# Recurrence of a two-block model: both head groups take the block inverse in step, on 32 columns

## The chip, the cores and the metric

One NeuronCore of a Trainium2 chip runs the whole program. The metric is the device time of one execution in microseconds (us), lower is better; a kernel is given by the median of several executions. PE is TensorE (PEld its loads of weights, the stationary operand), DVE is VectorE, ACT is ScalarE, POOL is GpSimd and SP is SyncE.

## The reference, cut to what matters

The model is a stack of four layers and then a second block, all on 512 tokens of 1024 channels. Only one piece of the second block is touched by the change, the RWKV-7 recurrence over 16 heads of 64 channels:

```python
def step(state, inp):
    r_t, w_t, k_t, v_t, a_t, b_t = inp
    sa = jnp.einsum('bhij,bhj->bhi', state, a_t)
    state = state * w_t[:, :, None, :] + sa[..., None] * b_t[:, :, None, :] \
        + v_t[..., None] * k_t[:, :, None, :]
    return state, jnp.einsum('bhij,bhj->bhi', state, r_t)
_, ys = lax.scan(step, jnp.zeros((B, H, N, N), jnp.float32), xs)
```

All the rest (the projections, the MLPs, the attentions, the norms) stays as it was.

## The kernel before, in words

**The whole.** Nearly all the time goes to large projections whose weights stream in and are split into an upper and a lower part (lines 435 and 440), and which PE multiplies in three float32r terms (line 505). Every engine runs one written-out program, and semaphores order them. The recurrence stands between the stage `g2` and the stage `mattn`: `pe_chunks`, `act_chunks`, `dve_chunks` and `pool_heads` (line 2216). No other work of PE runs inside it.

**The recurrence in chunks.** The 512 tokens are cut into 8 chunks (NC) of 64 (CH). Within a chunk the step by step scan becomes matrices of 64 by 64 for each head, and the sequential part becomes the inverse of a unit triangular matrix. The 16 heads lie as pairs (h, k): h is the half of the 128 partitions, k the column block 0 to 7. Group 0 is k = 0 to 3, group 1 is k = 4 to 7. Group 1 keeps its tokens in the other half of the partitions (`toks`, line 1875) than its channels (`chan`, line 1871), so that products of tokens into channels use the quadrants of PE's array that group 0 leaves free. `together` (line 1879) issues the products of one or more groups turn by turn. A float32 product is two instructions on PE, so one product for all the heads of a group is 16 matmuls, and for both groups 32.

**The inverse.** It is built by levels of doubling blocks. X and Z hold the inverse so far and its transpose. `first_x` and `first_z` (lines 1962 and 1963) make level 0, for blocks of 2. Level l = 1 to 5 does three products: `times` (line 1993) multiplies the masked matrix TM with X to give Y, `more_x` (line 1964) multiplies Z with Y and VectorE adds the result to X (`add_x`, line 2178), and `more_z` (line 1965) adds into Z's PSUM bank (6 and 2, ZB), which ScalarE copies to SBUF (`act_z`, line 2080). X and Y share the PSUM banks 4 and 5 (YX). ScalarE copies Y to SBUF as Yt (`act_y`, line 2084). Level 5 makes no X. The masks `mk` leave in TM only the source rows and target columns that join two neighbouring blocks of 2 to the power l, so a product has only 32 of 64 columns that change, but before the change all 64 are computed and copied.

**The order of the work.** The two groups go staggered: PE does `times` of group 0, then `more_x` and `more_z` of group 1 for the level before, then other work, then `more_x` of group 0, then `more_z` of group 0 with `times` of group 1. The other work lies in the middle of a level, while the copies of Y and Z run: at l = 1 the turning of the next chunk's V and B (`pe_turn`, line 1890), at l = 2 the head sums of the chunk before (line 1916) and `w0_tok` (line 1967), at l = 3 `w0_state` (line 1969) and the head spread (line 1924), at l = 4 the products with B of the next chunk (`pe_products`, line 1900), at l = 5 the turning of its K. After level 5 come U (line 1971), with the products with K of the next chunk between its two groups, then `o_v`, `ds_b`, `ds_k`, `o_u` and `o_state` (lines 1975, 1972, 1973, 1977, 1979). The next chunk's `first_x` follows at once; its `first_z` waits until ScalarE has copied the output out of ZB (semaphore `ck_out`, line 2127). The last chunk has no next one, and its levels 1, 4 and 5 lack the other work.

**VectorE in a chunk** copies X (line 2189), updates the state (`state`, lines 2173 to 2175), adds X, makes the masked TM (`level`, line 2151, 512 elements), masks the products with B (`mask_b`) and K (`mask_k`, both line 2146), makes the first level of the next chunk (lines 2163 and 2164), and scales the finished heads (line 1947). POOL then finishes those heads.

## Time and profile before

| what | value |
|---|---|
| median of 3 executions | 3448.69 us (3445.75 to 3448.97) |
| the profiled execution, its own time | 3444.75 us |
| its span in the profile | 3442.9 us |
| instructions | 51687 |
| granted TensorE clock, mean | 0.993 of full speed |
| PE, PEld busy | 98%, 80% of the span |
| DVE, ACT, POOL busy | 51%, 34%, 14% |
| the recurrence, from first_x of chunk 0 to the end of chunk 7 | 2633.5 to 2853.5 us |

The profile gives busy times per engine; matmuls overlap in their pipeline, so the busy time is the union of intervals and their ends are modelled. The timeline of the trace lists instructions in order of start with their count, and in brackets the idle time of that engine before them and what ended it. A start to start distance on PEld is the best clock for how fast PE goes through a burst of products.

### The profile page before, as it was taken

Reading aid. Unit: us, or ns where it says so; the run is one execution under the profiler, and the core shown is the slowest. Engines: PE = TensorE matmul, PEld = TensorE weight load, DVE = VectorE, ACT = ScalarE, POOL = GpSimd, SP = SyncE. Lnnn points to the kernel's source line nnn. Section 1 sums busy time; section 2 is a strip of 40 time slices with the busy share of each in tenths; the row PEclk is TensorE's granted clock in tenths of the full one; section 3 lists DMA queues with packets and bytes.
Section 4 is the critical chain, followed back from the end, with each engine's and each line's share of the span. In section 5 each row is a group of like instructions: output and inputs, shape, how many; then the busy total and the mean of one; then the engine's idle time right before and its main releaser. Section 6 shows DMA issues by size and latency. Waiting matters only on the chain. (4 is left out here: it accounts for less than half of the span.)

```text
span 3442.9 us, 51687 instructions
## 1 busy us (share of the span) xinstructions
PE 3368.9 (98%) x21556; PEld 2754.1 (80%) x21556; DVE 1754.3 (51%) x1916; ACT 1161.5 (34%) x1452; POOL 465.4 (14%) x420
## 2 busy tenths in 40 slices
PE   8999999999999999999999999999998989999998
PEld 6688888888888888888588888887777877878887
DVE  7764343454345554345765243555686554554342
ACT  3532223432222232222532123334663542342122
POOL 1011011020011021011011012100141221111011
PEclk9999999999999999999999999999999999999999
DMA  4233233232322233233233323343332122313232
GB/s 144 68 105 103 87 98 99 85 98 98 98 98 89 95 100 103 91 98 117 71 97 97 99 96 110 112 131 114 107 96 82 41 65 97 112 61 108 88 100 71
DMA packets 313223, 329.56 MB, mean 96 GB/s; under 512 B 22707, under 2 KB 303670, under 8 KB 312534
## 3 DMA queue, kind: packets, MB, share of 16 engines
q1 hardware_dynamic: 306069, 303.33, 27.7%
q0 software_dynamic: 4464, 19.40, 1.7%
q10 hardware_dynamic: 2512, 4.26, 0.3%
q8 instruction: 137, 2.24, 0.3%
q14 instruction: 41, 0.33, 0.0%
HBM read 312.28 MB, written 14.68 MB: 95 GB/s over the span
## 5 line engine op out<-in xcount | busy, mean ns | idle before, releaser
L505 PE MATMUL ps<-xh,wh 128*128 128x512 f32 x2360 | 930.7, 394 | 9.4 <-DVE wl L440 7.2
L505 PE MATMUL ps<-xh,wl 128*128 128x512 f32 x2360 | 920.3, 390 | 0.0
L505 PE MATMUL ps<-xl,wh 128*128 128x512 f32 x2360 | 919.9, 390 | 0.0
L440 DVE TENSOR_TENSOR wl<-raw,wh 128x2048 fp32r<-128x2048 f32 (+1 forms) x279 | 636.6, 2282 | 425.6 <-ACT wh L435 425.3
L435 ACT ACTIVATE wh<-raw 128x2048 fp32r<-128x2048 f32 (+1 forms) x281 | 526.2, 1873 | 639.8 <-PE ps L505 627.2
L505 PEld LDWEIGHTS ps<-xh,wh 128*128 128x128 f32 x2360 | 444.2, 188 | 114.5 <-issue 21.3
L505 PEld LDWEIGHTS ps<-xl,wh 128*128 128x128 f32 x2360 | 444.1, 188 | 95.6 <-issue 4.6
L505 PEld LDWEIGHTS ps<-xh,wl 128*128 128x128 f32 x2360 | 443.9, 188 | 92.9
L505 PE MATMUL ps<-hh,wh 128*128 128x512 f32 x1280 | 498.5, 389 | 1.1 <-DVE wl L440 0.9
L505 PE MATMUL ps<-hh,wl 128*128 128x512 f32 x1280 | 498.0, 389 | 0.0
L505 PE MATMUL ps<-hl,wh 128*128 128x512 f32 x1280 | 497.9, 389 | 0.0
L621 POOL TENSOR_TENSOR hf<-tmp 128x512 f32<-128x512 f32 x160 | 163.2, 1042 | 1133.7 <-DVE tmp L668 1133.7
L588 ACT ACTIVATE hh<-tmp 128x512 f32 (+1 forms) x160 | 97.8, 633 | 598.8 <-DVE tmp L668 598.8
L505 PEld LDWEIGHTS ps<-hh,wh 128*128 128x128 f32 x1280 | 240.3, 188 | 52.2 <-DVE wl L440 2.4
L505 PEld LDWEIGHTS ps<-hh,wl 128*128 128x128 f32 x1280 | 240.3, 188 | 49.7
L505 PEld LDWEIGHTS ps<-hl,wh 128*128 128x128 f32 x1280 | 240.3, 188 | 49.7
L668 DVE SCALAR_TENSOR_TENSOR tmp<-ps,rs 128x512 f32<-128x512 f32 x160 | 103.1, 686 | 341.3 <-PE ps L505 341.1
L679 DVE TENSOR_TENSOR x<-x,ps 128x512 f32 (+1 forms) x128 | 82.3, 684 | 355.8 <-PE ps L505 355.8
L634 POOL TENSOR_TENSOR acc<-acc,hf 128x512 f32<-128x512 f32 x80 | 118.5, 1481 | 1016.1 <-ACT hf L600 1012.2
L674 DVE TENSOR_TENSOR hl<-hf,hh 128x512 f32 (+1 forms) x160 | 158.5, 1029 | 55.3 <-POOL hf L621 55.3
L598 ACT ACTIVATE xh<-x,prm (+1 forms) x72 | 51.6, 717 | 273.5 <-DVE x L679 273.5
L505 PE MATMUL ps<-yh,wh 128*128 128x512 f32 x352 | 137.5, 391 | 0.0
(425 smaller groups left out, 3660.0 us busy)
## 6 DMA issues: line engine op xcount, KB each, us to landing
raw<-in_mlp_w SPq DMA_DIRECT2D x128, 1024.0 KB, 5.4
raw<-in_ffn_w SPq DMA_DIRECT2D x32, 1024.0 KB, 5.3
raw<-in_w_in SPq DMA_DIRECT2D x31, 1024.0 KB, 5.4
raw<-in_a_w_in SPq DMA_DIRECT2D x20, 1024.0 KB, 5.1
raw<-in_c_w_in SPq DMA_DIRECT2D x12, 1024.0 KB, 5.1
raw<-in_a_w_out SPq DMA_DIRECT2D x16, 640.0 KB, 4.0
raw<-in_b_w_in SPq DMA_DIRECT2D x8, 1024.0 KB, 5.8
raw<-in_xa_wkv SPq DMA_DIRECT2D x8, 1024.0 KB, 5.9
```

The lines of the kernel that those rows point to most:

```text
L435: nc.scalar.activation(wh[:, p.slot(su), 0:n], raw[:, p.slot(su), 0:n], ACT.Copy).then_inc(upper, 1)
L440: nc.vector.tensor_tensor(wl[:, p.slot(su), 0:n], raw[:, p.slot(su), 0:n], wh[:, p.slot(su), 0:n], ALU.subtract).then_inc(lower, 1)
L505: last = nc.tensor.matmul(banks[mt][:, 0:st.n], stat_, ops[oi][at_, kk, 0:st.n], start=k == 0 and su == 0 and n_ == 0, stop=k == kb - 1 an ...
L588: nc.scalar.activation(hh[:, bass.ds(t, 1)], tmp[:, mt:mt + 1, 0:T], ACT.Square).then_inc(acted, 1)
L598: nc.scalar.activation(xh[:, bass.ds(t, 1)], x[:, bass.ds(t, 1)], ACT.Copy, scale=gaincol(st, t)).then_inc(acted, 1)
L621: nc.gpsimd.tensor_tensor(hf[:, mt], tmp[:, mt, 0:T], tmp[:, mt, 0:T], ALU.mult).then_inc(pooled, 1)
L634: nc.gpsimd.tensor_tensor(acc[:], acc[:], sq[:, mt], ALU.add).then_inc(pooled, 1)
L668: nc.vector.scalar_tensor_tensor(out=tmp[:, mt, 0:T], in0=ps[b + mt][:], scalar=0.0, in1=rs[:], op0=ALU.max, op1=ALU.mult).then_inc(evac, 1)
L674: nc.vector.tensor_tensor(hl[:, bass.ds(t, 1)], hf[:, mt:mt + 1], hh[:, bass.ds(t, 1)], ALU.subtract).then_inc(split, 1)
L679: nc.vector.tensor_tensor(xt, xt, ps[b + mt][:].rearrange("p (a n) -> p a n", a=1), ALU.add).then_inc(evac, 1)
```

## The change

Levels of the inverse: both groups are taken in step. PE issues `times` of both groups, then the level's other work, then `more_x` of both, then `more_z` of group 0 and then of group 1. Before `times` it waits for X of both groups, before `more_x` for the copies of Y and Z of both. VectorE copies Y of group 1 (`copy_y`), ScalarE that of group 0. `times` and `more_x` stream 32 columns instead of 64 (`sides` picks every other block of 2 to the power l columns) and write 32 columns packed; `more_z` streams 32 and writes them to every other block of the PSUM bank. The copies and additions move 128 instead of 256 elements per partition; they scatter or gather by blocks. Y gets a tile of its own for each level (hf, Yt, gd twice, rs), and five memsets, four ahead of chunk 0's X and one in its level 3, clear them, since `more_z` loads all 64 columns of Y as weights. Moved are: the products with K of the next chunk, from between the two groups of U to behind the next chunk's own `first_x`, with `mask_k` after the X copies; the state update, from the start of a chunk to behind level 1's additions; `mask_b`, from level 4 to level 5; `level(c, l + 2)`, to between the copy of Y and the additions. The number of matmuls stays the same.

```diff
+    def sides(v, l, b):
+        return v.rearrange("p (m b i) -> p m b i", b=2, i=1 << l)[:, :, b]
+    def packed(v, l):
+        return v.rearrange("p (m i) -> p m i", i=1 << l)
+    YL = [None, hf[:, 1].rearrange("p (q n) -> p q n", n=CH), Yt[:]] + \
+        [gd[:, h].rearrange("p (q n) -> p q n", n=CH) for h in range(2)] + [rs[:].rearrange("p (q n) -> p q n", n=CH)]
...
             if c:
+                pe.wait_ge(s("ck_bmasked"), c + 1)
+                pe_products(pe, c, 1, "ck_kprod")
                 pe.wait_ge(s("ck_out"), c)
...
             for l in range(1, 6):
-                times = lambda h, k: mm(ps[YX[k // 4]][chan(h, k), cols(k)], TM[l % 2][toks(h, k), k], X[toks(h, k), k],
-                                        start=True, stop=True)
-                pe.wait_ge(s("ck_x0"), 5 * c + l)
+                times = lambda h, k: mm(packed(ps[YX[k // 4]][chan(h, k), k % 4 * 32:k % 4 * 32 + 32], l), TM[l % 2][toks(h, k), k],
+                                        sides(X[toks(h, k), k], l, 0), start=True, stop=True)
+                def more_x(h, k, l_):
+                    return mm(packed(ps[YX[k // 4]][toks(h, k), k % 4 * 32:k % 4 * 32 + 32], l_), Z[chan(h, k), k],
+                              sides(YL[l_][chan(h, k), k], l_, 0), start=True, stop=True)
+                def more_z(h, k, l_):
+                    return mm(sides(ps[ZB[k // 4]][chan(h, k), cols(k)], l_, 1), YL[l_][chan(h, k), k],
+                              sides(Z[chan(h, k), k], l_, 1), start=False, stop=True, skip_group_check=True)
...
+                for g in range(2):
+                    pe.wait_ge(s(f"ck_x{g}"), 5 * c + l)
                 pe.wait_ge(s("ck_tm"), 6 * c + l + 1)
-                together(group(0, times))[0].then_inc(s("ck_y0"), 1)
-                if l > 1:
-                    pe.wait_ge(s("ck_y_copied1"), 5 * c + l - 1)
-                    pe.wait_ge(s("ck_z1"), 6 * c + l - 1)
-                    last = together(group(1, more_x), group(1, more_z))
-                    last[0].then_inc(s("ck_xm1"), 1)
-                    last[1].then_inc(s("ck_zm1"), 1)
+                last = together(group(0, times), group(1, times))
+                last[0].then_inc(s("ck_y0"), 1)
+                last[1].then_inc(s("ck_y1"), 1)
...
-                pe.wait_ge(s("ck_y_copied0"), 5 * c + l)
-                pe.wait_ge(s("ck_z0"), 6 * c + l)
+                for g in range(2):
+                    pe.wait_ge(s(f"ck_y_copied{g}"), 5 * c + l)
+                    pe.wait_ge(s(f"ck_z{g}"), 6 * c + l)
                 if l < 5:
-                    together(group(0, more_x))[0].then_inc(s("ck_xm0"), 1)
-                pe.wait_ge(s("ck_x1"), 5 * c + l)
-                last = together(group(0, more_z), group(1, times))
-                last[0].then_inc(s("ck_zm0"), 1)
-                last[1].then_inc(s("ck_y1"), 1)
-            pe.wait_ge(s("ck_y_copied1"), 5 * c + 5)
-            pe.wait_ge(s("ck_z1"), 6 * c + 5)
-            together(group(1, more_z))[0].then_inc(s("ck_zm1"), 1)
+                    last = together(group(0, x_now), group(1, x_now))
+                    last[0].then_inc(s("ck_xm0"), 1)
+                    last[1].then_inc(s("ck_xm1"), 1)
+                together(group(0, z_now))[0].then_inc(s("ck_zm0"), 1)
+                together(group(1, z_now))[0].then_inc(s("ck_zm1"), 1)
             pe.wait_ge(s("ck_w0_copied"), 2 * c + 2)
             pe.wait_ge(s("ck_z0"), 6 * c + 6)
             together(group(0, u_of))[0].then_inc(s("ck_u"), 1)
-            if more:
-                pe.wait_ge(s("ck_bmasked"), c + 2)
-                pe_products(pe, c + 1, 1, "ck_kprod")
...
     def act_y(act, c, g, l):
         act.wait_ge(s(f"ck_y{g}"), 5 * c + l)
-        act.activation(half(Yt, g), half(b3(YX[g]), g), ACT.Copy).then_inc(s(f"ck_y_copied{g}"), 1)
+        act.activation(sides(half(YL[l], g).rearrange("p q n -> p (q n)"), l, 0), packed(ps[YX[g]][:, 0:P], l), ACT.Copy)\
+            .then_inc(s(f"ck_y_copied{g}"), 1)
...
+        def copy_y(c, l):
+            dve.wait_ge(s("ck_y1"), 5 * c + l)
+            nc.vector.tensor_copy(sides(half(YL[l], 1).rearrange("p q n -> p (q n)"), l, 0), packed(ps[YX[1]][:, 0:P], l))\
+                .then_inc(s("ck_y_copied1"), 1)
...
+        dve.wait_ge(s("bonus_stored1"), 64)
+        for l in range(1, 5):
+            nc.vector.memset(YL[l], 0.0)
...
             if c:
-                state(c - 1)
+                mask_k(c)
             for l in range(1, 6):
-                if l > 1:
-                    add_x(c, 1, l - 1)
+                copy_y(c, l)
+                if l < 4:
+                    dve.wait_ge(s("ck_y0"), 5 * c + l)
+                    level(c, l + 2)
                 if l < 5:
                     add_x(c, 0, l)
+                    add_x(c, 1, l)
+                if l == 1 and c:
+                    state(c - 1)
```

`act_z` is changed like `act_y` (every other block, from level 1 on), and `add_x` adds 128 packed elements into every other block of X.

## Rows read from the trace of the kernel before

**Rows 1.** The page: the span, and the busy time of each engine with its share and instructions.

```profile
span 3442.9 us, 51687 instructions
...
PE 3368.9 (98%) x21556; PEld 2754.1 (80%) x21556; DVE 1754.3 (51%) x1916; ACT 1161.5 (34%) x1452; POOL 465.4 (14%) x420
```

**Rows 2.** Stretches of the recurrence, all of it, then chunks 3, 4 and 7. Columns: window, length, then busy us and count of PE, PEld, DVE, ACT, POOL, granted clock, DMA share, GB/s.

```profile
2633.50:2853.50 220.00, 191.59 (x6872) 174.94 (x6872) 110.97 (x202) 108.10 (x284) 42.04 (x30) 0.98 0.19 49
...
2714.80:2742.00 27.20, 24.32 (x890) 22.27 (x888) 13.24 (x26) 13.41 (x37) 4.70 (x4) 1.00 0.16 43
2742.00:2769.00 27.00, 24.58 (x879) 22.41 (x877) 13.24 (x26) 13.20 (x37) 4.69 (x4) 1.00 0.16 43
...
2827.50:2853.50 26.00, 20.93 (x785) 18.81 (x781) 9.08 (x21) 12.19 (x35) 4.70 (x4) 0.99 0.17 51
```

**Rows 3.** PE's waits, chunks 1 to 6: who waited, us in total, times, longest.

```profile
PE ps L1962 <- issue: 5.2, 3, 2.4
PE ps L1965 <- ACT cYt L2086: 3.1, 6, 0.5
PE ps L1977 <- issue: 2.8, 2, 2.1
PE ps L1963 <- ACT VT L2127: 2.1, 3, 0.7
```

**Rows 4.** The same view for PE's weight loads.

```profile
PEld ps L1993 <- DVE cX L2180: 3.7, 19, 0.2
```

**Rows 5.** Timeline, the start of chunk 3 to its level 2. Columns: start us, duration us, engine, line.

```profile
2714.79 0.98 PE L1962 MATMUL ps<-i,hf 64*64 64x64 f32 x25
...
2714.99 1.55 ACT L2127 ACTIVATE VT<-ps 64x256 f32<-64x256 f32 x4 [3.46 <-PE ps L1979]
...
2717.24 0.60 PEld L1993 LDWEIGHTS ps<-cX,cTM 64*64 64x64 f32 x16
...
2717.90 0.30 PEld L1895 LDWEIGHTS ps<-c,VT 128*128 128x128 f32 x2
...
2718.20 0.69 DVE L2175 TENSOR_TENSOR cST<-cST,PCs 128x512 f32<-128x512 f32 x1
...
2718.23 0.30 PEld L1895 LDWEIGHTS ps<-c,VT 128*128 128x128 f32 x2
...
2719.43 0.54 PEld L1964 LDWEIGHTS ps<-cYt,cZ 64*64 64x64 f32 x16 [0.17 <-issue]
...
2720.16 0.42 DVE L2180 TENSOR_TENSOR cX<-cX,ps 128x256 f32<-128x256 f32 x1 [1.27 <-PE ps L1964]
...
2720.63 0.54 PEld L1993 LDWEIGHTS ps<-cX,cTM 64*64 64x64 f32 x16 [0.19 <-DVE cX L2180]
...
2721.75 0.97 PEld L1920 LDWEIGHTS ps<-headones,hs 128*128 128x128 f32 x8
...
2722.73 0.56 PEld L1967 LDWEIGHTS ps<-cVB,TLK 64*64 64x64 f32 x32
```

**Rows 6.** Timeline, the end of chunk 3's levels and its U.

```profile
2735.04 0.54 PEld L1965 LDWEIGHTS ps<-cZ,cYt 64*64 64x64 f32 x16 [0.66 <-ACT cYt L2086]
...
2735.51 0.55 PEld L1971 LDWEIGHTS ps<-cW,cZ 64*64 64x64 f32 x16
...
2735.78 0.38 ACT L2082 ACTIVATE cZ<-ps 128x256 f32<-128x256 f32 x1 [0.51 <-PE ps L1965]
2735.92 0.90 PEld L1904 LDWEIGHTS ps<-AR,KT 64*64 64x64 f32 x32
...
2736.74 0.48 PEld L1971 LDWEIGHTS ps<-cW,cZ 64*64 64x64 f32 x12
...
2737.15 1.29 DVE L2146 TENSOR_TENSOR TLK<-ps,acc 128x512 f32<-128x512 f32 x2 [0.93 <-PE ps L1904]
```

**Rows 7.** Groups of instructions on DVE that give the price of smaller copies and of a memset.

```profile
L1439 DVE SCALAR_TENSOR_TENSOR sc<-dist,ps 128x128 f32<-128x128 f32 x32 | 7.7, 281 | 0.0
...
L2137 DVE MEMSET cST<- 128x512 f32 x1 | 0.5, 485 | 0.2 <-issue 0.2
```

More of the change, by code:

```diff
@@ L1963, in pe_chunks @@
             first_z = lambda h, k: mm(ps[ZB[k // 4]][chan(h, k), cols(k)], i64[toks(h, k), :], TI[toks(h, k), k], start=k % 4 == 0, stop=True, skip_group_check=True)
-            more_x = lambda h, k: mm(ps[YX[k // 4]][toks(h, k), cols(k)], Z[chan(h, k), k], Yt[chan(h, k), k], start=True, stop=True)
-            more_z = lambda h, k: mm(ps[ZB[k // 4]][chan(h, k), cols(k)], Yt[chan(h, k), k], Z[chan(h, k), k],
-                                     start=False, stop=True, skip_group_check=True)
             w0_tok = lambda h, k: mm(ps[WB[k // 4]][chan(h, k), cols(k)], TLK[b][toks(h, k), k, 0], Vt[b][toks(h, k), turned(h, k)],
@@ L2081, in act_z @@
         act.wait_ge(s(f"ck_zm{g}"), 6 * c + l + 1)
-        act.activation(half(Z, g), half(b3(ZB[g]), g), ACT.Copy).then_inc(s(f"ck_z{g}"), 1)
+        to, of = half(Z, g).rearrange("p q n -> p (q n)"), ps[ZB[g]][:, 4 * g * CH:4 * g * CH + 4 * CH]
+        if l:
+            to, of = sides(to, l, 1), sides(of, l, 1)
+        act.activation(to, of, ACT.Copy).then_inc(s(f"ck_z{g}"), 1)
     def act_y(act, c, g, l):
         act.wait_ge(s(f"ck_y{g}"), 5 * c + l)
-        act.activation(half(Yt, g), half(b3(YX[g]), g), ACT.Copy).then_inc(s(f"ck_y_copied{g}"), 1)
+        act.activation(sides(half(YL[l], g).rearrange("p q n -> p (q n)"), l, 0), packed(ps[YX[g]][:, 0:P], l), ACT.Copy)\
+            .then_inc(s(f"ck_y_copied{g}"), 1)
     EARLY_SPLIT = {1: At(stages["mattn"], 0, 0, 0), 5: At(stages["merge"], 0, 0, 0)}
@@ L2106, in act_chunks @@
                     act_turned_vb(act, c + 1, PB)
-                if l > 1:
-                    act_z(act, c, 1, l - 1)
                 if l == 2 and c:
@@ L2116, in act_chunks @@
                     act_turned_k(act, c + 1)
-                act_y(act, c, 1, l)
-                act_z(act, c, 0, l)
-            act_z(act, c, 1, 5)
+                for g in range(2):
+                    act_z(act, c, g, l)
             for g in range(2):
@@ L2165, in first_levels @@
             if c:
+                dve.wait_ge(s("ck_y0"), 5 * c)
                 dve.wait_ge(s("ck_y1"), 5 * c)
@@ L2176, in state @@
                 .then_inc(s("ck_state"), 1)
+        def copy_y(c, l):
+            dve.wait_ge(s("ck_y1"), 5 * c + l)
+            nc.vector.tensor_copy(sides(half(YL[l], 1).rearrange("p q n -> p (q n)"), l, 0), packed(ps[YX[1]][:, 0:P], l))\
+                .then_inc(s("ck_y_copied1"), 1)
         def add_x(c, g, l):
             dve.wait_ge(s(f"ck_xm{g}"), 5 * c + l + 1)
-            nc.vector.tensor_tensor(half(X, g), half(X, g), half(b3(YX[g]), g), ALU.add).then_inc(s(f"ck_x{g}"), 1)
+            to = sides(half(X, g).rearrange("p q n -> p (q n)"), l, 0)
+            nc.vector.tensor_tensor(to, to, packed(ps[YX[g]][:, 0:P], l), ALU.add).then_inc(s(f"ck_x{g}"), 1)
         mask_b(0)
@@ L2200, in dve_chunks @@
                     dve_head_scale(dve, c - 1)
-                if l < 4:
-                    dve.wait_ge(s("ck_y1"), 5 * c + l)
-                    level(c, l + 2)
-                if l == 4 and more:
+                if l == 3 and c == 0:
+                    dve.wait_ge(s("g_stored1"), 64)
+                    nc.vector.memset(YL[5], 0.0)
+                if l == 5 and more:
                     if c == 0:
@@ L2209, in dve_chunks @@
                 first_levels(c + 1)
-                mask_k(c + 1)
         state(NC - 1)
```

3 lines of the change are left out of this document (2 added, 1 removed).

## The prediction, made before the changed kernel ran

> **What bounds the kernel now.** I read the page first: PE is busy for 98% of a span of 3442.9 us [rows 1], so only what shortens PE's own path counts. The recurrence is the one part in which PE does small products and waits for copies. The stretches of the windows view [rows 2] show its size: 220.0 us, 6.4% of the span, about 27 us for a chunk, with PE busy 191.6 us. At most 28 us are idle in it, and nothing outside it is touched. The clock granted there is 0.98 to 1.00, the upper level of 2.4 GHz, so the clock is no part of the sum.
>
> Next, who PE waits for in chunks 1 to 6. Matmul rows [rows 3] name ScalarE's copy of Y (3.1 us in 6 waits), ScalarE's output copy VT ahead of `first_z` (2.1 us in 3) and "issue", time for which the profile has no releaser, ahead of `first_x` (5.2 us in 3) and `o_u` (2.8 us in 2). The weight loads [rows 4] show 19 small waits, 0.19 us each, of `times` for X. These rows hold about 17 us. They are small waits because the staggered groups already cover each other: while a copy of one group runs, PE multiplies for the other.
>
> Last, the pace of PE inside a level, from the timeline [rows 5]. From 2719.43 to 2720.63 there are two bursts (`more_x` of group 0 with 16 matmuls, then `more_z` of group 0 with `times` of group 1, 32 matmuls) and 0.19 us idle: 1.01 us for the two, 0.50 us each, whether a burst has 16 matmuls on two quadrants of the array or 32 on four. 16 loads of 0.134 us fill 0.54 us, so the loads of one quadrant start (0.54 - 0.13) / 7 = 0.058 us apart.
>
> **Part 1, the bursts themselves.** Before, a chunk has per level `times` of group 0, `more_x` and `more_z` of group 1, `more_x` of group 0, and `more_z` of group 0 with `times` of group 1, and at the end a lone `more_z`: 5 + 4 + 4 + 5 + 1 = 19 bursts. After it has 5 of `times`, 4 of `more_x` and 5 times two of `more_z`, which is 19 again. `times` and `more_x` gain by filling four quadrants, but `more_z` of both groups lies in the same two quadrants (it goes from channels to channels) and can't be paired, so it gives that gain back. Bursts: 0 us.
>
> **Part 2, 32 columns instead of 64.** No row has a 64 by 64 float32 stationary with 32 moving columns. Bound from above: nothing changes, 0.058 us a step. Bound from below: the streaming halves, 0.029 us. The nearest row is the head sums, 128 by 128 stationary with only 2 moving columns [rows 5]: 8 loads in 0.97 us, (0.97 - 0.19) / 7 = 0.111 us apart. The transposed V next to it, same stationary and 128 moving columns, runs three instructions in 2718.23 - 2717.90 = 0.33 us, 0.110 us apart. Going from 128 columns to 2 gave nothing there, so the load of the stationary sets the step, and 64 loaded columns at that rate need 0.056 us, just what is seen now. I take 0 us, and keep the other end as a rival. A DVE operation of 128 elements out of PSUM takes 281 ns [rows 7] where the addition to X takes 0.42 us [rows 5]. I take 0.14 us less for the copies of ScalarE too (no row; between nothing and half of its 0.38 us). Blocks of 2 floats in the strided tiles could make these slower; the copies have cover, so a loss of up to 0.1 us each changes nothing.
>
> **Part 3, a level in step.** After `times` PE needs the end of the pipeline (0.2 us), a copy (0.28) and hand-offs, some 0.6 us. In chunks 0 to 6 the level's other work stands there: it is 1.53 us at level 1 (2717.90 to 2719.43 [rows 5]), 0.97 + 0.46 at level 2, more at level 3 (`w0_state` of both groups, then the spread), 0.8 at level 4 (products as large as those with K [rows 6]), some 0.5 at level 5. DVE's `level` of 0.69 us now stands ahead of the additions, but ends inside that work too. After `more_x` come the two bursts of `more_z`, 1.0 us, and in that time DVE does both additions: 0.2 + 0.05 + 0.19 + 0.28 + 0.05 = 0.77 us. So the 0.19 us ahead of `times` goes, 4 times a chunk: -0.76 us. At level 5 the lone `more_z` waited 0.66 us for Y [rows 6]; now U waits for the copy of Z instead, behind ScalarE's turned K (two copies, 0.66 us, on its queue ahead of both Z copies), some 0.35 us. Net -0.31 us.
>
> **Part 4, the products with K.** Between the groups of U they hold PE from 2735.92 to 2736.74, 0.82 us and a hand-off [rows 6]: -0.9 us. In the new place they stand in the shadow of the four VT copies (2714.99 to 2716.54 [rows 5]), which was there anyway, so they add nothing. But `mask_k`, 1.29 us on DVE [rows 6], now runs after them, and the turning at level 1 waits for it, because it writes the banks that the mask reads. Counted from the start of `first_x`: 0.92 for it, 0.9 for the products, 0.25 hand-off, 1.29, makes 3.4 us; the turning now starts at 3.1 us (2714.79 to 2717.90 [rows 5]). +0.3 us. Queued behind `mask_k` on DVE is the copy of Y for level 1, which is needed only after the turning. SP's two loads for the finished heads wait on the same products and start some 7 us later; their POOL readers come at level 4, and I see cover for them.
>
> **Part 5, the other moves.** `state` (0.41 + 0.41 + 0.69 us with overlap, 1.45) now runs after the additions of level 1. Its reader `w0_tok` comes 0.5 + 1.0 us after `times` of level 2 starts; just covered, 0 us, up to 0.3 if not. `mask_b` at level 5 delays the first level of the next chunk to some 4 us ahead of `first_x`; 0 us. Four memsets of 485 ns [rows 7] stand once between the masks of chunk 0 and its copy of X, with nothing else for PE to do: +1.8 us. The fifth is covered.
>
> **The sum.** A full chunk: -0.76 - 0.31 - 0.9 + 0.3 = -1.7 us. Chunks 1 to 6: -10.2. Chunk 0: -2.0 (no K mask inside it) + 1.8 = -0.2. Chunk 7 has no other work at levels 1, 4 and 5, so the 0.6 us behind `times` stands bare there, about what its waits are now (26.0 us with PE busy 20.9 [rows 2]): 0. Then the cover that is gone: 3 of the "issue" stalls stand at `first_x` [rows 3], where the VT wait (0.85 us when nothing else stalls) hid part of each; with the products there, 3 x 0.85 = 2.6 us come out. -10.4 + 2.6 = -7.8 us. The profiled execution took 3444.75 us, 3.9 below the median of 3448.69; against its own time the sum gives 3437.0, and against the median 3440.9 us.
>
> **Rivals.** Something under 0.2%, 6.9 us, a measurement of this kernel can hardly tell from no change.
>
> *A, 32 columns pay.* If a step falls from 0.058 to 0.029 us, a burst loses 8 x 0.029 = 0.23 us, 19 x 8 bursts 35 us. The additions (0.77 us) then outlast two `more_z` (0.52), which takes back 0.25 x 4 x 8 = 8 us. That is 27 us on top: about 3414; halfway, 3427. Against it stand the head sums. The Trainium skill (TensorE: Matmul & The Clock Gate, Back-to-back issue gap) gives a warm gap of N/2.4 + 2.5 ns, and by it alone the time would be this rival's. Chance 0.17.
>
> *B, the gain is given back.* The stalls named "issue" come at no fixed place, 8 of the 17 us of waits. PE issues the same instructions, in less time; if they are due to how fast instructions come, they grow by what is saved. Or the level 1 chain of part 4 grows with each stall at `first_x`. About 3447. Chance 0.20.
>
> *C, slower: the scattered write of `more_z`.* At level l it writes runs of 2 to the power l floats into PSUM, which no product of before does. There are 10 bursts a chunk, 80 in all. If each took twice its 0.46 us, 37 us would come on top: 3478. It decides from 0.1 us a burst on, where it eats the forecast. Against it: the shortest run is 8 bytes, and only level 1 has it. The Trainium skill (Advanced Engine Details and Errata, Memory Cachelines) says that a non-contiguous PSUM pattern significantly slows matmuls, and that pairs of elements should be contiguous; no row here shows a case. Chance 0.09.
>
> *D, slower: VectorE's queue.* With `mask_k`, `level`, `state` and the copy of Y in one row, a late mask holds the copy for both groups, and PE has no other group to turn to. 1.5 us a chunk beyond the forecast's cover would give 3453. Chance 0.06.
>
> **Numbers.** The forecast has 0.48, of which a fifth ends within 0.2%. Faster: 0.38 + A 0.17 = 0.55. Same: 0.10 + B 0.20 = 0.30. Slower: C + D = 0.15. The range from 3418 to 3452 leaves out the far half of A, all of C and part of D.
>
> **What would show it.** Right: `first_x` to `first_x` some 25.3 us in chunks 3 and 4; weight loads of 64 by 64 with 32 columns still 0.055 to 0.06 us apart; no wait of `times` on X; the products with K right behind `first_x`; U behind a short wait for Z. Wrong: steps under 0.05 us (A); `more_z` bursts over 0.6 us (C); rows in which PE waits for DVE's Y or mask at over 0.5 us a chunk (D), or "issue" over 20 us in the recurrence (B).

## The result, and the profile after

Over 20 runs of each, the changed kernel takes 3452.86 us (3444.86 to 3460.53) and the kernel before 3447.22 us (3444.07 to 3450.23): ratio 1.0016, 95% interval 1.001 to 1.0022. That is 5.6 us slower where 7.8 us less was forecast, and 0.9 us outside the range. It is also inside the 0.2% called "no change" in advance, but 20 runs a side resolve it.

The profiled execution of after took 3460.53 us, the slowest of its runs. Its page and stretches:

```profile
span 3458.7 us, 51699 instructions
PE 3376.5 (98%) x21556; PEld 2763.4 (80%) x21556; DVE 1755.4 (51%) x1961; ACT 1138.2 (33%) x1412; POOL 463.3 (13%) x420
```

Windows view of after: the whole recurrence, then chunks 1, 3, 4 and 7, each from its copy of X to that of the next (chunk 7 to the recurrence's end; columns as in [rows 2]).

```profile
2639.80:2870.60 230.80, 196.89 (x6872) 183.99 (x6872) 110.68 (x244) 83.95 (x241) 39.30 (x30) 0.92 0.18 47
2668.60:2696.80 28.20, 23.81 (x880) 21.75 (x878) 17.50 (x32) 13.43 (x34) 8.85 (x5) 1.00 0.16 42
2723.90:2751.90 28.00, 24.63 (x878) 23.09 (x876) 12.94 (x32) 10.28 (x32) 4.32 (x4) 0.94 0.16 42
2751.90:2779.70 27.80, 23.48 (x879) 21.74 (x875) 13.25 (x32) 10.39 (x32) 4.31 (x4) 1.00 0.16 42
2838.90:2870.60 31.70, 25.41 (x808) 23.83 (x804) 9.39 (x25) 8.36 (x26) 4.31 (x4) 0.78 0.35 103
```

The recurrence has 6872 matmuls as before. Measured alike it took 219.1 us before and 230.8 here, 11.7 more; it also began 6.3 us later. That shift is no part of the change: late_w_b and fewer_instr below, which have before's order of work, begin at 2639 or 2640 too, others of the changed order at 2633. It goes with the clock ahead of the recurrence, in work that no kernel here touches: 20 us at a granted clock of 0.50 just before it in after, late_w_b and fewer_instr, 10 us in before. So this trace overstates the loss, and each cause below is priced by timed runs.

Chunk 4 is 27.8 us long at a clock of 1.00, with PE busy for 23.48 us in 879 matmuls; before's had 24.58 busy of 27.0 us, in 879 too [rows 2]. So in this chunk there is less work, and more idle time. The prediction wanted 25.3 us from `first_x` to `first_x` in chunks 3 and 4; they take 28.0 and 27.9. Chunk 7, cut alike 24.6 us before, takes 31.7 us at a clock of 0.78. Three things changed. The first is in PE's waits, chunks 1 to 6, the view of [rows 3] (who waited, us in total, times, longest):

```profile
PE ps L1980 <- issue: 4.4, 3, 1.9
PE ps L2010 <- issue: 4.3, 6, 1.3
PE ps L1984 <- issue: 2.7, 2, 1.9
PE ps L1986 <- issue: 1.9, 1, 1.9
PE ps L2006 <- issue: 1.9, 3, 1.0
PE ps L1905 <- DVE TLK L2158: 1.8, 4, 0.5
PE ps L2002 <- issue: 1.5, 3, 0.8
```

The waits for the copies are mostly gone, as planned (ScalarE's copy of Y ahead of `more_z`, 3.1 us before, and VT, 2.1 us). But "issue" has grown and has spread to `ds_k` (L1980), `more_z` (L2010), `o_u` (L1984) and `more_x` (L2006). Over the whole recurrence, PE's weight loads wait for ScalarE 5.8 us (13.2 before), for VectorE 6.1 (5.0), for "issue" 33.2 (23.8).

The second is the clock. Stretches of 5 us inside the recurrence of after:

```profile
2780.00:2785.00 5.00, 3.97 (x125) 3.47 (x118) 2.68 (x6) 4.24 (x8) 0.00 (x0) 1.00 0.50 107
2785.00:2790.00 5.00, 4.65 (x176) 4.48 (x170) 2.85 (x8) 1.83 (x6) 0.00 (x0) 0.88 0.03 5
2790.00:2795.00 5.00, 5.00 (x103) 4.88 (x103) 1.37 (x5) 1.60 (x5) 0.00 (x0) 0.50 0.01 3
2795.00:2800.00 5.00, 4.79 (x186) 4.47 (x184) 1.86 (x6) 0.83 (x3) 2.18 (x2) 0.93 0.02 3
```

At 0.50, the lower level of 1.2 GHz, a stretch holds 103 matmuls where its neighbours at or near the upper level hold 176 and 186. With a mean clock of 0.92, 37 of the 231 us ran at the lower level (twice 0.08, times the length), against 7 before (mean 0.984). The timed runs say the same of the whole span: its mean clock was 0.988 to 0.992 in the 20 runs of after, 0.990 on average, and 0.993 in before's profiled one.

The third was foreseen: the memsets ahead of chunk 0's copy of X. Timeline of VectorE (start us, duration us):

```profile
2642.15 0.48 DVE L2206 MEMSET hf<- 128x512 f32 x1
2642.69 0.48 DVE L2206 MEMSET cYt<- 128x512 f32 x1
2643.23 1.02 DVE L2206 MEMSET gd<- 128x512 f32 x2
2644.18 0.68 DVE L2211 COPY cX<-ps 128x256 f32<-128x256 f32 x2
```

They cost 2.0 us, and PE waits for that copy (PEld L2002 <- DVE cX L2211, 3.6 us, once).

### The profile page after: what moved, and what is told of

It reads as the page before. It is cut to its first block and busy times, and to the rows that moved or that the text cites. A ratio compares the mean times of both kernels' runs of the same rounds, so it can differ in the third digit from the quotient of the medians.

```text
span 3458.7 us, 51699 instructions
## 1 busy us (share of the span) xinstructions
PE 3376.5 (98%) x21556; PEld 2763.4 (80%) x21556; DVE 1755.4 (51%) x1961; ACT 1138.2 (33%) x1412; POOL 463.3 (13%) x420
## 3 DMA queue, kind: packets, MB, share of 16 engines
q1 hardware_dynamic: 306069, 303.33, 27.8%
```

## What a stall named "issue" is

This came from lining up PE's weight loads with the DMA queue view's packets of kind "instruction". The end of chunk 2 and the start of chunk 3 in after, weight loads, with what they waited for:

```profile
2719.28 0.54 PEld L1980 LDWEIGHTS ps<-cVB,cKt 64*64 64x64 f32 x27
2721.62 0.14 PEld L1980 LDWEIGHTS ps<-cVB,cKt 64*64 64x64 f32 x3 [1.79 <-issue]
...
2723.03 1.05 PEld L1972 LDWEIGHTS ps<-i,hf 64*64 64x64 f32 x32
2723.95 0.86 PEld L1914 LDWEIGHTS ps<-AR,KT 64*64 64x64 f32 x27
2725.47 0.14 PEld L1914 LDWEIGHTS ps<-AR,KT 64*64 64x64 f32 x3 [0.66 <-issue]
```

The DMA view from 2718 to 2728 us (GB/s in 40 slices of 0.25 us), and its queue rows:

```profile
GB/s 459 377 197 33 66 0 0 0 0 0 0 0 0 0 0 0 0 0 66 0 0 0 0 0 0 0 0 0 0 0 0 0 0 0 0 2 138 132 190 271
...
q8 instruction: 3, 0.05, 2.5%
```

Three packets of 16 KB (0.05 MB) in 10 us. The single slices of 66 GB/s (16 KB in 0.25 us) are two of them: 2719.0 and 2722.5. By the packets' own records the first starts at 2719.1, 2.5 us before PE goes on at 2721.62, and the second at 2722.7, 1.1 us after that.

PE's stalls, in every trace, lie 126.5 weight loads or a multiple of that apart. Each load has its matmul, so that is 253 instructions, and with the few others among them (waits that stand alone) some 256 to a packet of 16 KB. The counts agree: 6872 loads and 6872 matmuls over before's 54 packets are 254 each.

A *block* is from here on the work between two such boundaries. It ends in a *stall* if the last weight load before a boundary and the first one behind it start more than 0.45 us apart, whatever the profile names as the releaser. In before 18 of 53 blocks end in a stall of over 0.45 us (21.0 us in all), in after 27 of 53 (31.3 us). Where PE stalled, the packet had started 2.63 us before PE went on (standard deviation 0.26) in before and 2.51 (0.21) in after. It starts on average 1.1 us after the last boundary in blocks without a stall, and 1.6 (before) to 1.8 us (after) in blocks with one.

Hence the picture that the runs below test: **each block has a floor.** The next packet starts only when the present block is under way, and PE has it 2.5 us later; a block that PE gets through sooner waits out the rest. Time lost in one block is not made up in another.

A rival is a fixed price for each boundary, whatever PE does in the block. The traces settle that. Take as a block's own time its length without the step over the boundary at its end; all 212 blocks of before, after, and the pair late_w_b and combo_z below:

| own time of the block | blocks | with a stall | mean length, us |
|---|---|---|---|
| under 3.0 us | 62 | 53 | 3.9 |
| 3.0 to 3.5 us | 57 | 31 | 3.8 |
| 3.5 to 4.0 us | 44 | 6 | 4.0 |
| 4.0 us and more | 49 | 8 | 4.7 |

The lighter the block, the longer the stall, and the length stays at 3.8 to 4.0 us. Of its 53 blocks, before has 26 with under 3.5 us of their own, late_w_b 26 and stagger32, also in the old order, 28; after has 32 and combo_z 35. The changed order makes blocks lighter, and light blocks stall.

The Trainium skill (Runtime: NRT & Kernel Launch, Instruction fetch mechanics) has the same blocks, 16 KiB or 256 instructions, and says that the next is fetched while the current one executes and that the crossing is mostly hidden. The traces agree on the size. They do not on the hiding: 10% of before's recurrence are such stalls.

## Experiments

Times are medians, ratios are against the kernel before on the same chip in the same rounds, with 95% intervals. Most medians are of 11 executions (5 for more_instr and more_time, 6 for early_w, 20 for after). Most intervals are 3 us to either side, so a difference of 2 or 3 us between two of these kernels is not resolved by its timed runs. "Recurrence" columns are of the one profiled execution of each: length, PE busy, not busy (the difference), "issue" waits of the weight loads, mean clock.

| kernel | us | before | ratio | length | busy | idle | issue | clock |
|---|---|---|---|---|---|---|---|---|
| before | | | | 219.1 | 191.6 | 27.5 | 23.8 | 0.98 |
| after | 3452.86 | 3447.22 | 1.0016 (1.001, 1.0022) | 230.8 | 196.9 | 33.9 | 33.2 | 0.92 |
| stream64 | 3451.22 | 3448.12 | 1.0008 (0.9999, 1.0017) | 227.5 | 189.4 | 38.1 | 38.5 | 0.97 |
| z64 | 3450.36 | 3448.12 | 1.0009 (1.0, 1.0018) | 225.4 | 189.1 | 36.3 | 35.3 | 0.96 |
| step64 | 3451.74 | 3448.12 | 1.0011 (1.0002, 1.002) | 228.0 | 192.9 | 35.1 | 34.8 | 0.97 |
| stagger32 | 3451.99 | 3448.12 | 1.0013 (1.0004, 1.0022) | 228.9 | 199.9 | 29.0 | 26.8 | 0.92 |
| k_back | 3450.19 | 3442.55 | 1.0016 (1.0007, 1.0025) | 228.7 | 195.3 | 33.4 | 30.4 | 0.93 |
| more_instr | 3458.28 | 3442.55 | 1.0043 (1.003, 1.0056) | 232.3 | 190.7 | 41.6 | 38.1 | 0.99 |
| fewer_instr | 3443.58 | 3442.55 | 1.0001 (0.9993, 1.001) | 219.4 | 190.4 | 29.0 | 25.8 | 0.98 |
| early_w | 3456.85 | 3442.55 | 1.0036 (1.0024, 1.0048) | 228.1 | 196.6 | 31.5 | 31.0 | 0.92 |
| late_w_b | 3441.14 | 3446.01 | 0.9987 (0.9978, 0.9996) | 216.8 | 189.4 | 27.4 | 23.5 | 1.00 |
| late_w_a | 3447.86 | 3446.01 | 1.0005 (0.9996, 1.0015) | 222.7 | 193.8 | 28.9 | 27.9 | 0.93 |
| more_time | 3465.15 | 3445.15 | 1.0054 (1.004, 1.0068) | 241.8 | 215.8 | 26.0 | 38.4 | 0.96 |
| fewer3 | 3440.16 | 3445.15 | 0.9984 (0.9975, 0.9993) | 210.4 | 184.3 | 26.1 | 19.7 | 0.98 |
| combo_b | 3443.29 | 3445.15 | 0.9997 (0.9988, 1.0006) | 218.1 | 189.5 | 28.6 | 24.6 | 0.98 |
| combo_z | 3440.81 | 3445.15 | 0.9991 (0.9982, 1.0) | 217.5 | 183.9 | 33.6 | 35.0 | 0.99 |

### The order alone, the columns alone

**stream64**: the changed order, products over 64 columns, copies still of 128.

```diff
-                times = lambda h, k: mm(packed(ps[YX[k // 4]][chan(h, k), k % 4 * 32:k % 4 * 32 + 32], l), TM[l % 2][toks(h, k), k],
-                                        sides(X[toks(h, k), k], l, 0), start=True, stop=True)
+                times = lambda h, k: mm(ps[YX[k // 4]][chan(h, k), cols(k)], TM[l % 2][toks(h, k), k], X[toks(h, k), k], start=True, stop=True)
...
```

> The changed order, with times, more_x and more_z streaming and writing all 64 columns again; the copies and additions still move 128 elements. Theory 1 (clock): the recurrence of the changed kernel has a mean granted clock of 0.91 because its products stream half the columns; with 64 the clock is back at 0.98 or more there and the time is 8 to 12 us under the kernel before (about 3437). Theory 2 (order): VectorE's queue and the issue stalls eat the gain of the step order; the time stays 3 to 8 us above the kernel before, whatever the width.

**z64**: the changed kernel, only `more_z` back at 64 columns.

```diff
-                    return mm(sides(ps[ZB[k // 4]][chan(h, k), cols(k)], l_, 1), YL[l_][chan(h, k), k],
-                              sides(Z[chan(h, k), k], l_, 1), start=False, stop=True, skip_group_check=True)
+                    return mm(ps[ZB[k // 4]][chan(h, k), cols(k)], YL[l_][chan(h, k), k],
+                              Z[chan(h, k), k], start=False, stop=True, skip_group_check=True)
```

> The changed kernel with only more_z at 64 columns (10 of the 19 bursts of a chunk), times and more_x at 32. Theory 1 (clock): part of the columns are back, so the clock in the recurrence lies between 0.91 and 0.98 and the time between that of the changed kernel and that of stream64. Theory 2 (order): same time as the changed kernel. Rival C (the scattered write of more_z is slow): this run alone brings most of the gain, by shorter more_z bursts at the full clock.

**step64**: the changed order with nothing narrowed, products and copies of before's size, without the four memsets ahead of chunk 0.

```diff
-            nc.vector.tensor_copy(sides(half(YL[l], 1).rearrange("p q n -> p (q n)"), l, 0), packed(ps[YX[1]][:, 0:P], l))\
+            nc.vector.tensor_copy(half(YL[l], 1), half(b3(YX[1]), 1))\
...
-        for l in range(1, 5):
-            nc.vector.memset(YL[l], 0.0)
```

> The changed order with nothing narrowed: 64 columns in the products, 256 elements in the copies and additions, no memsets. Theory 1: 0 to 4 us faster or slower than stream64 (memsets 1.8 us less, the copies of 0.42 us instead of 0.28 mostly covered), so also 6 to 12 us under the kernel before. Theory 2: some 5 us above the kernel before.

**stagger32** (its edit against before): before's order, with the 32 columns, the small copies and the memsets.

```diff
-                    last = together(group(1, more_x), group(1, more_z))
+                    last = together(group(1, x_old), group(1, z_old))
...
+        dve.wait_ge(s("bonus_stored1"), 64)
+        for l in range(1, 5):
+            nc.vector.memset(YL[l], 0.0)
...
```

> The order of before (groups staggered, ScalarE copies both Y) with products, copies and additions on 32 columns, and the memsets. Theory 1 (clock): the granted clock in the recurrence falls as in the changed kernel, and the time is 5 to 15 us above the kernel before. Theory 2 (order): no worse than before apart from the 1.8 us of memsets, minus some us for shorter copies: -5 to +2 us.

All four lie above before, by 2.8 to 4.5 us by their ratios, though the intervals of stream64 and z64 reach down to no difference. All overlap: neither half of the change alone is seen to gain anything. For stream64 the theory of the clock alone had promised 8 to 12 us under before; that did not come, and the 3 to 8 us above, by the order, came at their lower end.

The traces separate them where the times can't. The three with the changed order have 34.8 to 38.5 us of "issue", stagger32 with the old one 26.8. Over all traces with before's amount of work, the five in the old order (before, late_w_b, fewer_instr, combo_b, stagger32) have 23.5 to 26.8 us, the eight in the changed one 27.9 to 38.5.

The two with 32 columns everywhere (after, stagger32) have a clock of 0.92 in the recurrence; `more_z` over 64 columns alone brings it to 0.96. Here the timed runs agree. The mean clock of the whole span, averaged over all executions of a kernel, is 0.989 to 0.991 in the five kernels with 32 columns everywhere (after, stagger32, k_back, early_w, late_w_a), and 0.992 to 0.994 in all the others and in before in each of the four later rounds. So the order makes the stalls, and the 32 columns make the clock fall, in either order. Why narrow products do that was not tried.

The lower clock costs less than it looks. Part of the slower work falls into time that PE would have spent waiting: after has 33.2 us of "issue" where stream64 has 38.5. After and z64 differ by 0.0007, 2.4 us, within their intervals.

### Where the K products stand

**k_back**: the changed kernel, with the K products and their mask back between the groups of U.

```diff
             if c:
-                pe.wait_ge(s("ck_bmasked"), c + 1)
-                pe_products(pe, c, 1, "ck_kprod")
                 pe.wait_ge(s("ck_out"), c)
...
             together(group(0, u_of))[0].then_inc(s("ck_u"), 1)
+            if more:
+                pe.wait_ge(s("ck_bmasked"), c + 2)
+                pe_products(pe, c + 1, 1, "ck_kprod")
```

> The changed kernel with the products with K of the next chunk (and their mask) back between the two groups of U. Theory 3: PE's instruction supply sets the pace of the chunks, so this too stays within 3 us of the changed kernel, but the weights that SP fetches behind chunk 7's slices come 7 us earlier, at the end of chunk 6, and chunk 7 is 2 to 4 us shorter than the 33 us of the changed kernel. Rival (the K mask ahead of the turning and the copy of Y costs PE time in each chunk): 3 to 6 us faster than the changed kernel, from chunks 1 to 6.

Ratio 1.0016, that of after. The waits for ScalarE come back (9.3 us against 5.8), the "issue" waits shrink (30.4 against 33.2). Part 4's 0.6 us a chunk, 4 us in all, do not show, with intervals that leave some 3 us to either side: they move from one name to the other. The shorter chunk 7 that was expected did not come: it takes 32.6 us from its copy of X to the end, with the weights' loads under way from 2825.6 to 2835.6, across its start.

### Does the number of instructions cost time?

**more_instr**: before, each B and K product in two halves of 64 columns.

```diff
-            return mm(ps[PB[k // 4]][toks(h, k), k % 4 * P:k % 4 * P + P], (BT, KT)[which][at_, c, own(h, k)],
-                      AR[at_, c, own(h, k)].rearrange("p a n -> p (a n)"), start=True, stop=True)
+            return mm(ps[PB[k // 4]][toks(h, k), k % 4 * P + 64 * half_:k % 4 * P + 64 * half_ + 64], (BT, KT)[which][at_, c, own(h, k)],
+                      AR[at_, c, own(h, k), half_], start=True, stop=True)
...
```

> The kernel before, with each product of pe_products (64 by 64 stationary, 128 moving columns, a step of 0.11 us) split into two of 64 columns (2 steps of 0.057 us): the same PE time, 512 more weight loads and 512 more matmuls, which is 4 more spans of 256 instructions (the stalls named issue stand every 126 weight loads in all six traces). Theory 3 (PE's instructions arrive late, about one such span per 3.5 to 4 us, and the stalls are that): +6 to +15 us, all of it issue time in the recurrence. Rival (the stalls are something else, a fixed cost or a drain): +0 to +2 us.

```profile
2633.80:2866.10 232.30, 190.73 (x7320) 173.95 (x7320) 110.42 (x199) 107.40 (x281) 41.99 (x30) 0.99 0.18 47
```

448 more matmuls are in the window than in before's, PE is busy 190.73 us, no longer than in before (191.59), and the recurrence is 13.2 us longer; the whole 15 us (0.0043 of 3443). Four packets' worth of instructions that add no work cost 3.8 us each. That is a direct price of instructions: the trace has 57 blocks of 4.03 us on average where before has 53 of 4.02.

**fewer_instr**: before, `first_z` as 4 products of 256 columns.

```diff
-            last = together(group(0, first_z), group(1, first_z))
+            last = []
+            for g in range(2):
+                for h in range(2):
+                    ins = mm(ps[ZB[g]][HP[h], 4 * g * CH:4 * g * CH + 4 * CH], i64[toks(h, 4 * g), :],
+                             TI[toks(h, 4 * g), 4 * g:4 * g + 4].rearrange("p q n -> p (q n)"), start=True, stop=True, skip_group_check=True)
...
```

> The kernel before, with first_z as 4 products of 256 moving columns instead of 16 of 64 (same stationary, the same streamed columns): 192 weight loads and 192 matmuls fewer in all, 1.5 spans of 256 instructions. Theory 3: -3 to -6 us. Rival: 0, within 1.5 us.

A miss: nothing gained. A supply that only has a mean pace would have paid for 384 instructions. This is what turned "a pace for all" into "a floor for each block". Its trace has 52 blocks of 4.10 us where before has 53 of 4.02: there is one block less, and the others are fuller. Why adding instructions costs 3.8 us a packet where taking them out brings nothing was not followed further.

**more_time**: before, with 32 idle products over 512 columns.

```diff
+        for q in range(2):
+            mm(ps[PB[0]][HP[0], :], i64[HP[0], :], AR[HP[0], c, 4 * q:4 * q + 4].rearrange("p q a n -> p (q a n)"), start=True, stop=True)
         together(group(0, product), group(1, product))[-1].then_inc(s(done), 1)
```

> The kernel before, with two idle products ahead of each of the 16 calls for B and K (64 by 64 identity, 512 moving columns, into a bank that the call then overwrites): 32 products, 128 PE instructions or half a packet, but some 0.43 us of PE work each (128 columns take 0.11 us), 13.7 us in all. Supply theory (about 256 instructions per 3.9 us): PE falls behind and the packets catch up, so the 'issue' waits shrink by most of what is added: recurrence longer by 2 us for the half packet and up to 6 in all, 'issue' waits from 24 to under 15 us. Rival (PE's own work and the copies' waits set the pace, and the issue waits are a price of their own): 12 to 14 us more, ratio 1.0038, issue waits as before. The same count of instructions against more_instr, which added 1024 instructions and no work and cost 15 us.

The expectation mis-sized the added work: each product is two matmuls, and the trace has one of 512 columns at 589 ns against 269 for one of 128, 0.83 ns a column, so 0.43 us for each of 64 and not for each of 32: 27 us. PE busy grew by 24.2 us in the recurrence, the length by 22.7, the whole by 18.6 us (0.0054). So between a sixteenth (22.7 of 24.2, in the trace) and a third (18.6 of 27, in the timed runs) was absorbed, and the rest came on top.

```profile
PEld ps L1964 <- issue: 9.6, 4, 2.5
PEld ps L1907 <- issue: 8.3, 28, 0.3
PEld ps L1904 <- issue: 7.3, 28, 0.3
```

The second and third rows are loads that wait for the long matmuls ahead of them. Without those, the issue waits are 22.8 us, as good as before's 23.8: the four stalls of `first_x` (L1964, up to 2.5 us) still stand. PE was 23 us slower, and the supply did not run ahead in that time. That refutes the theory with a mean pace (under 15 us of issue waits, at most 6 longer). A fixed price for each boundary would do as well here; against it stands the table of the blocks above, and here too all 9 blocks with under 3.0 us of their own stall, and 2 of the 37 with 3.5 us and more.

**fewer3**: before, leaving out 12 of 16 K products of chunks 1 to 7, and 14 of 16 `o_u` products of each chunk, so the mask products with K and the output are incomplete.

```diff
+        if c and which:
+            for k in range(0, NH2, 4):
+                last = product(0, k)
+                last = product(1, k)
...
-            together(group(0, o_u), group(1, o_u))[1].then_inc(s("ck_crossed"), 1)
+            o_u(0, 7)
+            o_u(1, 7).then_inc(s("ck_crossed"), 1)
```

> The kernel before, with 12 of the 16 K products of chunks 1 to 7 and 14 of the 16 o_u products of each chunk left out: 84 + 112 = 196 products, 784 PE instructions, 3.06 packets. PE's work shrinks by 7 x 0.6 + 8 x 0.44 = 7.7 us. Supply theory: 3.06 x 3.9 = 12 us less, ratio 0.9965. Rival (PE's own work): 7.7 us or less, since part of the work covers copies and their waits come out, ratio 0.998 or above. Under 3 us less would say with fewer_instr, which gained nothing, that the path runs through the copies.

5.5 us less (0.0016), the recurrence 8.7 less in its trace, PE busy 7.3 less, "issue" 4.1 less: by the size PE's own work suffices, and the 12 us expected of a mean pace are not there. One stall (2.87 us) now even tops the longest of before.

### The loads of the next weights

Behind the slices for chunk 7, SP loads the weights of the projection that follows, two times 1 MB. In before they start at 2820.9, beside the end of chunk 6 (2797.5 to 2828.0, 30.5 us long against 27); in after at 2841.3, beside chunk 7 (31.7 us to the recurrence's end; the expectations' 33.2 us is a stretch cut some 4 us early, 2834.5 to 2867.7).

**early_w**: the changed kernel, the two loads behind the slices of chunks 2 and 5.

```diff
                 if st.kind == "merge" and p.c == 1:
                     sp_g(sp)
-                    sp_slices(sp)
+                    sp_slices(sp, 0, 3)
+                if st.kind == "merge" and p.c == 2:
+                    sp_slices(sp, 3, 6)
...
```

> The changed kernel with the two loads of 1 MB of weights behind the recurrence's slices issued earlier, one behind the slices of chunk 2 and one behind those of chunk 5, instead of both behind those of chunk 7. Theory 3 with contention (an instruction fetch waits behind the weights): chunk 7 loses its stall of 1 to 3.5 us, and chunks 3 and 6 take 1 to 2 us each more; the total within 2 us of the changed kernel. Rival (chunk 7 is long for the bare levels 1, 4 and 5 alone): chunk 7 stays at 32 to 33 us.

**late_w_b** and **late_w_a**: before and after, the loads behind the last chunk.

```diff
                     sp_slices(sp)
+                    sp.wait_ge(s("ck_yout"), NC)
```

> The kernel before, with SP waiting for the last chunk's output before it issues the two 1 MB loads of the projection's weights, which otherwise run beside chunk 6 (30.5 us long against 27 for the others). If the burst slows the instruction packets in its chunk: chunk 6 back to 27, 2 to 4 us less in the recurrence, and nothing lost behind it if the weights come in time (2 MB at the rate seen take some 10 us): ratio 0.999. Rival, the chunk is long for reasons of its own, or the merge then waits for the weights: 0, or up to 5 us more.

> The changed kernel, with the same later loads. There they run beside chunk 7, 33.2 us long against 28 for the others. Contention theory: chunk 7 at some 29 us, 3 to 5 us less than the changed kernel, so back at the time of before (ratio 1.000). Rival: chunk 7 stays over 32 us, because it has no other work behind its copies (what the order in step brings with it), and the ratio stays at 1.0016.

early_w is slower still (0.0036, where at most 2 us on top of after were expected), and chunk 6, beside its second load, takes 34.1 us, at a mean clock of 0.75, while chunk 7 falls to 28.2: the long chunk follows the load. Put behind the recurrence, the loads bring 4.5 us in before (0.9987; that is a kernel faster than both) and 3.8 us in after (1.0005 against 1.0016, whose intervals overlap). So the burst costs about 4 us in before, and after's runs agree with that. It explains most of the long chunk 7 (27.9 us in late_w_a, still at a clock of 0.82), and chunk 6 of late_w_b is 28.5 us.

The traces show how a load that carries none of the recurrence's data comes to cost PE time: one instruction packet starts late. In before the packet of the block from 2824.8 starts 3.9 us after the block began, and the block lasts 6.5 us; in after the packet of the block from 2841.7 starts 4.9 us in, and the block lasts 7.3 us, the longest of either trace. Stream64, z64, step64, stagger32 and k_back have the same, one block beside the load of 6.5 to 7.8 us with its packet 3.8 to 5.1 us in. With the loads behind the recurrence (late_w_b, late_w_a, combo_z), no packet starts more than 3.3 us in, and no block is over 5.8 us. The first load of early_w, at 2697.0, did no harm: its three blocks take 3.7 to 4.2 us.

The burst does not explain the difference between the kernels, which is 0.0016 with the burst and 0.0018 without. Nothing is lost behind the recurrence: PE's waits there are the same in late_w_b as in before, 2.5 us for VT the largest.

### Adding up

**combo_b**: late_w_b with fewer_instr's `first_z`.

> The kernel before, with the projection's weights loaded behind the recurrence (late_w_b, 0.9987) and first_z as 4 products of 256 columns (fewer_instr, 1.0001, 384 instructions fewer). If the burst of loads had hidden what fewer instructions bring: 1.5 packets, up to 6 us below late_w_b, ratio 0.997. Otherwise the same as late_w_b: 0.9987.

0.9997 (0.9988 to 1.0006): the intervals of both overlap, but no gain shows on top of late_w_b. Fewer instructions at `first_z` are not seen to buy anything, with the burst or without.

**combo_z**: the changed kernel with late loads, `more_z` over 64 columns, and the memsets ahead of the mask of B.

```diff
+                    sp.wait_ge(s("ck_yout"), NC)
...
+        dve.wait_ge(s("bonus_stored1"), 64)
+        for l in range(1, 5):
+            nc.vector.memset(YL[l], 0.0)
         mask_b(0)
         first_levels(0)
         mask_k(0)
...
```

> The changed kernel with three things taken back: the loads of the weights behind the recurrence (late_w_a was 3.8 us under the changed kernel), more_z over 64 columns (z64 was 2.4 us under it, and the clock stayed at its upper level), and the four memsets ahead of the mask of B of chunk 0 (1.8 us of bare wait). If the three add up: 1.0016 - 0.0023 = 0.9993, so 2.3 us under before and 2 us above late_w_b, which has the old order. If only the loads count: 1.0005. If the order in step is worth something once its side costs are gone: under 0.9987.

0.9991 (0.9982 to 1.0) against 0.9993 expected: the side costs add up. Against late_w_a, which has the loads moved too, the memsets and `more_z` over 64 columns are worth 0.0014, 4.8 us. The clean pair is now late_w_b (old order) and combo_z (new order), neither with a burst, both at the upper clock. Windows view of the two recurrences:

```profile
2639.20:2856.00 216.80, 189.37 (x6872) 172.07 (x6872) 110.17 (x199) 107.09 (x282) 42.04 (x30) 1.00 0.16 41
```

```profile
2633.40:2850.90 217.50, 183.87 (x6872) 170.78 (x6872) 107.57 (x240) 84.15 (x241) 39.33 (x30) 0.99 0.16 40
```

The new order saves 5.5 us of PE's work (189.37 to 183.87) and 9.4 us of the waits for ScalarE and VectorE (19.1 to 9.7, of the weight loads, which overlap PE's work in part), and its "issue" waits go from 23.5 to 35.0. PE's idle time grows from 27.4 to 33.6 us and eats the 5.5. The two lengths agree within 0.7 us, and the two ratios within 0.0004, 1.4 us, though the intervals would leave room for 3 us to either side of each. combo_z's waits:

```profile
PEld ps L1981 <- issue: 6.4, 4, 2.2
PEld ps L2011 <- issue: 4.8, 8, 1.0
PEld ps L1915 <- issue: 4.3, 5, 1.3
PEld ps L1985 <- issue: 3.9, 2, 2.5
PEld ps L2007 <- issue: 3.7, 16, 0.8
PEld ps L1987 <- issue: 3.5, 2, 1.8
PEld ps L2003 <- issue: 3.3, 5, 1.2
```

## Why the prediction was wrong

**What bounds the kernel.** Right that PE's path in the recurrence is what counts, and that the copies' waits are small. "So the clock is no part of the sum" was wrong: it was read off the kernel before, and the change altered what PE does. And the 8 us of waits without a releaser were the largest rows of chunks 1 to 6 alone. Over the whole recurrence the weight loads of before already wait 23.8 us for "issue", of 27.5 us in which PE is idle. So "issue over 20 us", named as the sign of rival B, held before the change too and could not tell.

**Part 1 and part 2.** The pace of the bursts held. A level of chunk 1 in after, at the upper clock:

```profile
2674.15 0.56 PEld L2006 LDWEIGHTS ps<-hf,cZ 64*64 64x64 f32 x32 [0.41 <-ACT hf L2100]
2674.61 0.96 PEld L2010 LDWEIGHTS ps<-cZ,hf 64*64 64x64 f32 x30
...
2675.52 0.57 PEld L2002 LDWEIGHTS ps<-cX,cTM 64*64 64x64 f32 x30
```

`more_x` of both groups takes 0.46 us to the next burst and the two `more_z` 0.91, 0.057 us a step as before: the loads still set the step, so rival A (32 columns pay) fell, and C (scattered writes) too, with no burst over 0.6 us at the upper clock. PE's busy time fell all the same, by 5.5 us between late_w_b and combo_z, where Part 1 had 0. What part 2 costed at nothing has a price all the same: with 32 columns the granted clock falls, worth 2 to 3 us (after against z64: 2.4).

**Part 3 and part 4.** The mechanism was right: `times` no longer waits for X except once in chunk 0, and the K products stand in VT's shadow; the loads' 5.0 us of waits for the additions to X are gone, and their waits for ScalarE fell by 7.4 us. D (VectorE's queue) shows as 2.5 us in 5 waits of the turning for the mask, under 0.5 us a chunk.

**Part 5.** The memsets: 1.8 us forecast, 2.0 seen.

**The step that failed** is in the sum, "the cover that is gone": 3 stalls times 0.85 = 2.6 us. It took the "issue" stalls as things of fixed length that a wait may or may not hide. They aren't: a stalled PE goes on some 2.5 us after the start of the packet, whatever it waited for before, so what a light block loses in copies' waits it gets back as stall. Measured over the recurrence, "issue" grew by 9.4 us in after and by 11.5 between late_w_b and combo_z, where 5.5 us of work and 9.4 of other waits were saved. That is rival B ("the gain is given back"), which was named with a chance of 0.20 and its mechanism ("they grow by what is saved"), but as a weaker case than the forecast. B gave 3447, and before's median is 3447.22: a gain of nothing. Of the 5.6 us on top, the memsets are 2 and the clock 2 to 3; combo_z, which is rid of both and of the burst, comes out within 1.4 us of late_w_b.

What is shown: instructions without work cost 3.8 us a packet (more_instr); light blocks stall and full ones don't (the table of the blocks); the pair late_w_b and combo_z has the same length with less work in one; kernels with 32 columns everywhere have the lower mean clock, averaged over their runs. What stays open: why the packet starts 1.1 to 1.8 us after the boundary and not earlier, why narrow products bring the clock down, and why 384 instructions less bring nothing. The size of the clock's cost, 2 to 3 us, is a difference within the intervals. No run moved single instructions across a boundary.

## What to carry to other kernels

Where PE does many small products, count its instructions per microsecond before counting its waits. At 256 instructions in under 3.5 us, waits removed come back under the name "issue". Fewer instructions alone bought nothing here (fewer_instr), fewer with less work did (fewer3, 5.5 us). A wait without a releaser that recurs at equal counts of instructions is such a floor. Look at where large loads land beside such a stretch; moving two of them behind it gave the only complete kernel whose interval lies clear below before, 0.9987 (0.9978 to 0.9996).

## What the runs showed of the hardware

- The instruction packets: 16 KB each, 54 in the 219 us of before's recurrence; 2.6 us (deviation 0.3) in before and 2.5 (0.2) in after from the start of a packet to PE's going on; 21 us of stalls over 0.45 us in before. Blocks with under 3.5 us of their own last 3.8 to 3.9 us.
- A load of 2 MB beside the recurrence costs PE about 4 us though it moves none of the recurrence's data: 4.5 and 3.8 us gained when it goes. One instruction packet starts 3.9 (before) and 4.9 us (after) after its block began, instead of 1.1 to 1.8.
- The granted clock fell to 0.50 in a stretch with PE busy 5.00 of 5 us, when products of 64 by 64 had 32 moving columns; with `more_z` over 64 columns the recurrence's mean went from 0.92 to 0.96, and to 0.99 with the loads gone and the memsets moved. Over all timed runs the span's mean is 0.989 to 0.991 with 32 columns everywhere, 0.992 to 0.994 otherwise.
- A float32 matmul of 64 by 64 takes 269 ns with 128 columns and 589 ns with 512.
